# Attention heads of a two-block model: two waits of TensorE moved behind seven steps of projection, and the softmax division moved from VectorE to ScalarE

## The reference, cut to what matters

```
for layer in range(2):
    xn = rmsnorm(h, norm_mix[layer])
    if kind == 0:   # forget-gate attention, causal, with a bias c_q - c_k
        q, k, v, f_logit, qm = split(xn @ w_in_fox)
        p = softmax(q k^T * scale + c_q - c_k, masked)
    else:           # rotary positions, three dilated branches in one mask
        q, k, v, qm = split(xn @ w_in_dil)
        q, k = apply_rope(q), apply_rope(k)
        ...
    heads = concatenate([p @ v, memory_attention(qm, mem)])
    h = h + merge_heads(heads) @ w_out[layer]
    h = h + conv_ffn(rmsnorm(h, norm_ffn[layer]), ...)
```

## Time and profile before

| | |
|---|---|
| median of 3 timed runs | 2222.05 us (2220.85 to 2223.23) |
| the profiled execution's own time | 2216.38 us |
| its span | 2214.6 us |
| PE busy | 2099.2 us, 95% of the span |
| DVE busy | 1290.1 us, 58% |
| ACT busy | 466.4 us, 21% |
| POOL busy | 844.8 us, 38% |
| share of PE in the chain that ended last | 76%, of DVE 13%, of DMA 7% |

### The profile page before, as it was taken

How to read it: one execution, slowest core, us unless ns; L and a number is a source line. 1 busy time by engine, 2 the same in 40 slices (tenths; PEclk the granted TensorE clock), 3 DMA queues, 4 the chain that set the end, 5 groups by cost and what they waited for, 6 DMA issues and landing times.

```text
span 2214.6 us, 27273 instructions
## 1 busy us (share of the span) xinstructions
PE 2099.2 (95%) x10722; PEld 1669.6 (75%) x10722; DVE 1290.1 (58%) x1798; ACT 466.4 (21%) x852; POOL 844.8 (38%) x1008
## 2 busy tenths in 40 slices
PE   6999898998899999989999999999899999999996
PEld 4778786676788888867777888888676678888885
DVE  7686664448662342574565763727546757637274
ACT  3013301213210000123333210202233432102011
POOL 1333323233444444433222444444422324444442
PEclk7999999999999999999999999999999999999998
DMA  8978776589998988866665889898776648899885
GB/s 285 206 176 190 146 144 143 115 222 244 247 237 187 194 194 196 191 147 153 128 138 132 189 181 203 192 193 181 173 152 133 131 110 188 189 198 193 193 188 123
DMA packets 124615, 394.40 MB, mean 178 GB/s; under 512 B 26028, under 2 KB 28076, under 8 KB 124232
## 3 DMA queue, kind: packets, MB, share of 16 engines
q0 software_dynamic: 96480, 346.20, 72.5%
q1 hardware_dynamic: 28008, 46.45, 6.6%
HBM read 385.63 MB, written 3.94 MB: 176 GB/s over the span
## 4 chain that ended last, share of the span: by engine, by line
PE 76%; DVE 13%; DMA 7%; issue 1%; ACT 1%; SPq 1%; POOL 1%; DVEq 0%; ACTq 0%
PE ps L1674 65%; DMA w_lo<-in_w 4%; PE ps L1703 2%; PE ps L1870 2%; PE ps L1897 1%; PE ps L1883 1%; DMA arena<-in_ada 1%; DMA w_hi<-in_w 1%; DVE work L754 1%; PE ps L2062 1%; DVE small L927 1%; DVE arena L755 1%; DVE arena L637 1%; DVE arena L925 1%; POOL w_lo L497 1%
## 5 line engine op out<-in xcount | busy, mean ns | idle before, releaser
L1674 PE MATMUL ps<-h_hi,w_hi 128*128 128x512 f32 x1760 | 710.9, 404 | 36.6 <-DVE arena L862 14.4
L1674 PE MATMUL ps<-h_lo,w_hi 128*128 128x512 f32 x1760 | 690.7, 392 | 0.0
L1674 PE MATMUL ps<-h_hi,w_lo 128*128 128x512 f32 x1760 | 690.6, 392 | 0.0
L491 POOL DMA_DIRECT2D w_hi<-in_w x334 | 186.6, 559 | 1166.8 <-PE ps L1674 1032.3
L1674 PEld LDWEIGHTS ps<-h_hi,w_hi 128*128 128x128 f32 x1760 | 333.4, 189 | 129.3 <-issue 25.1
L1674 PEld LDWEIGHTS ps<-h_hi,w_lo 128*128 128x128 f32 x1760 | 333.1, 189 | 71.6
L497 POOL TENSOR_SCALAR w_lo<-w_hi 128x1024 fp32r<-128x1024 f32 (+1 forms) x334 | 360.0, 1078 | 69.5 <-DMA w_hi<-in_w 64.0
L1674 PEld LDWEIGHTS ps<-h_lo,w_hi 128*128 128x128 f32 x1760 | 333.8, 190 | 65.7 <-issue 1.9
L500 POOL DMA_DIRECT2D w_lo<-in_w x334 | 300.5, 900 | 105.8 <-POOL w_lo L497 105.8
L1674 PE MATMUL ps<-g_hi,w_hi 128*128 128x512 f32 (+1 forms) x728 | 286.1, 393 | 8.4 <-DMA w_lo<-in_w 6.1
L1674 PE MATMUL ps<-g_lo,w_hi 128*128 128x512 f32 (+1 forms) x728 | 281.5, 387 | 0.0
(11 more groups left out here) (376 smaller groups left out, 2134.4 us busy)
## 6 DMA issues: line engine op xcount, KB each, us to landing
w_hi<-in_w POOLq DMA_DIRECT2D x318, 512.0 KB, 3.9
w_lo<-in_w POOLq DMA_DIRECT2D x318, 512.0 KB, 5.6
arena<-in_ada SPq DMA_DIRECT2D x40, 512.0 KB, 8.2
w_hi<-in_w POOLq DMA_DIRECT2D x16, 384.0 KB, 3.3
w_lo<-in_w POOLq DMA_DIRECT2D x16, 384.0 KB, 5.0
x<-in_ada SPq DMA_DIRECT2D x8, 512.0 KB, 4.5
arena<-forget_sums SPq DMA_DIRECT2D x6, 512.0 KB
work<-arena SPq DMA_DIRECT2D x48, 64.0 KB, 3.3
```

Source lines behind the costliest of these rows:

```text
L491: pool.dma_start(w_hi[:, q % SLOTS, 0:n], A["w"][q][:, 0:n]).then_inc(S(f"high_in{q % SLOTS}"), 16)
L1674: mm = pe.matmul(bank, w[:, slot, cols], a(k), start=(k == 0 and i == 0), stop=(k == blocks - 1 and i == 2))
```

## The change: what it does

1. PE runs 7 steps (42 matmuls: all of q0, three quarters of k0) before it waits for banks 2 and 3, and `FIRST_STEPS` is (7, 4) in place of (2, 4). Five units lose their third step for it: 13, 17, 21, 25 and 29. The sum of the steps is 86 as before.
2. With that count q0 and k0 are both done "before unit 0". Their eviction has a new place, `evicted(-1)`, behind `top_of(0)` on DVE and behind `exponents(0)` on ACT; in the loop the evictions keep their place.
3. The wait for the mask is joined to the wait for the rotary table on DVE: both transfers now count on one semaphore, and the waits of DVE and PE on `mask_in` are gone.
4. The two multiplications of `divided` go from DVE (L935) to ACT, as Copy with a scale read per partition. DVE keeps the reciprocal and signals it. On ACT the division of unit u+1 stands behind `kept(u)`.

```diff
-FIRST_STEPS = (2, 4)
+FIRST_STEPS = (7, 4)
-    return 3 if u < 11 or u % 4 == 1 else 2
+    return 3 if u < 11 else 2
...
-            sp.dma_start(masks, A["mask_dil"]).then_inc(S("mask_in"), 16)
+            sp.dma_start(masks, A["mask_dil"]).then_inc(S("rope_in"), 16)
...
                 def divided(u):
-                    pair, qb, width, at = UNITS[u]
-                    pr, row = probs[u % P_SETS], small[:, 33 + u % P_SETS, :]
+                    row = small[:, 33 + u % P_SETS, :]
                     need("exped")
-                    do(dve.reciprocal(row[:, 2:4], row[:, 4:6]))
-                    for g in range(2):
-                        do(dve.tensor_scalar(pr[:, g, 0:width], pr[:, g, 0:width], row[:, 2 + g:3 + g], None, ALU.mult), "probs")
+                    do(dve.reciprocal(row[:, 2:4], row[:, 4:6]), "sums_turned")
...
                 top_of(0)
+                evicted(-1)
                 divided(0)
...
+                def divided(u):          # ScalarE
+                    width, row = UNITS[u][2], small[:, 33 + u % P_SETS, :]
+                    need("sums_turned")
+                    for g in range(2):
+                        pr = probs[u % P_SETS][:, g, 0:width]
+                        do(act.activation(pr, pr, ACT.Copy, scale=row[:, 2 + g:3 + g]), "probs")
...
                 exponents(0)
+                evicted(-1)
+                divided(0)
                 for u in range(len(UNITS) + 2):
...
+                    if u:
+                        evicted(u - 1)
                     if u < len(UNITS):
                         kept(u)
+                    if u + 1 < len(UNITS):
+                        divided(u + 1)
...
-                for at in (2, 3):
-                    pe.wait_ge(S(freed[at][0]), freed[at][1])
-                if layer:
-                    pe.wait_ge(S("mask_in"), 16)
                 steps = beside()
                 for _ in range(FIRST_STEPS[0]):
                     next(steps)
+                for at in (2, 3):
+                    pe.wait_ge(S(freed[at][0]), freed[at][1])
                 scores(0)
```

More of the change, by code:

```diff
@@ L852, in vector_layer @@
                 else:
-                    dve.wait_ge(S("rope_in"), 16)
+                    dve.wait_ge(S("rope_in"), 32)
                     for i in (2, 3):
@@ L867, in rotated @@
                     t, u = turn_room(1, i), work[:, 4, :]
-                    dve.wait_ge(S("rope_in"), 16 + 64 * (ROPED.index(name) + 1))
+                    dve.wait_ge(S("rope_in"), 32 + 64 * (ROPED.index(name) + 1))
                     do(dve.tensor_tensor(u, u, work[:, 3, :], ALU.mult))
@@ L904, in vector_layer @@
                 before = len(UNITS) * layer
-                if layer:
-                    dve.wait_ge(S("mask_in"), 16)
                 def pair_low(pair):
@@ L946, in beside, with evicted @@
                                 rotated(name)
+                    if u:
+                        evicted(u - 1)
+                def evicted(done):
                     for name, at in zip(BESIDE_PIECES, DONE_AT):
-                        if u == at + 1:
+                        if at == done:
                             if name[0] == "v":
@@ L1610, in kept, with evicted @@
                     do(act.activation(at_m["pt"][:, u % 2, :, 0:width], banks8[:, 4:6, 0:width], ACT.Copy), "probs_kept")
+                def evicted(done):
+                    for name, at in zip(BESIDE_PIECES, DONE_AT):
+                        if at == done:
+                            if name[0] == "v" or layer == 0:
+                                skip(1)
+                            else:
+                                rope_copy(name)
+                def divided(u):
[4 more added lines that the diff above has]
+                        do(act.activation(pr, pr, ACT.Copy, scale=row[:, 2 + g:3 + g]), "probs")
                 exponents(0)
+                evicted(-1)
+                divided(0)
                 for u in range(len(UNITS) + 2):
```

## The result

The changed kernel takes 2230.56 us (median of 5, 2226.07 to 2236.06) against 2223.23 for the kernel before beside it: 1.0039 times the time before, 95% interval 1.0024 to 1.0054. That is slower, where a gain of 8.3 us was forecast. The profiled execution is the shortest of the five, 2226.07 us; its span is 9.4 us longer than before.

What follows compares the result with a forecast made beforehand. PE's own work plus holes was taken as the bound. Layer 0 -9.3 us and layer 1 +1.0 sum to -8.3: 2208.1 for the profiled execution, 2213.7 us as timed median; own range 2210 to 2218, with rivals' bounds 2207 to 2221.

Steps and rivals of the forecast that it cites:

- (e): Layer 1 middle: idle from q and k swap waits and 512-wide units, 3.4 us again, so a change of 0.
- (d): Layer 1 middle: PE's clock falls once to its 1.2 GHz level behind a stall, +1.7 us (bounds 0 and 3).
- (b): Layer 1 middle: v0's first step waits for bank 0, freed by ACT's copy of q0 behind exponents(0), +2.5 us.
- (c): Layer 1 middle: q0 and k0 swapped back to back in loop 2, delaying unit 3's transposes, +4.4 us (bounds 3 and 6).
- (a): Layer 1 middle: three projection steps fewer, -4.2 us; the same -4.2 was booked in layer 0's middle.
- Layer 0's head: From PE's first possible projection step to scores(0): 42 matmuls fill the hole, scores(0) at 993.4 instead of 997.38, -4.0 us.
- the rule weighed in the prediction: DVE's divisions: two-port VectorE tensor_scalar and GpSimd lock each other out; moving them to ACT takes such blocks away.
- Layer 0's tail: From scores(25) to the last head block: two steps ahead -2.8, kept and slower division +1.0, together -1.8 us.
- The two steps ahead: Layer 0's tail: PE arrives with 70 steps done in place of 68, -2.8 us.
- ACT's price of the division: Division on ACT: 0.722 us for a 512-wide pass and 0.509 for 256, taken from Exp rows; DVE needs 0.491.
- ACT becomes the bound: Rival, chance 0.08: PE-ACT loop over 48 mixing units; 0.26 us more each is over 0.2% slower, 0.4 us ends at 2233.
- the gain is given back: Rival, chance 0.20: swap meets POOL, clock falls after both stalls; layer 1 costs 5, layer 0 gives 7: 2220 us.

Runs made afterwards that it cites:

- the second profile of the change: The unaltered change measured once more beside the kernel before, on the chip of that call: 2229.71 us, 1.0038 of the kernel before.
- the swaps' edit: The full change with a second buffer for the swapped halves, used in turn: 2217.34 us, 0.9983 of the kernel before.

## Why the prediction was wrong

**The step that failed** is (e) of layer 1's middle: "q1, k1, q2, k2 meet theirs in three-step loops with room", put down at 0. Each of these loops was costed by one question, whether the transposes of the probabilities would be late. But the count sets the evictions too. Before, v1 and v2 were evicted in loops 6 and 10, k1 and k2 rotated in loops 7 and 11. Now k1 is rotated and v1 evicted in loop 5, k2 and v2 in loop 9. The eviction is written behind the rotation, and PE's next projection but one waits for its bank. Before, v1's eviction stood behind a rotation too, that of q1 in loop 6, but q1's swap had landed and DVE didn't wait for it; the wait came a loop later, for k1, behind the eviction. DVE before:

```profile
1655.97 0.69 DVE L871 TENSOR_TENSOR arena<-arena,work 128x512 f32<-128x512 f32 x1
1656.69 0.69 DVE L877 TENSOR_TENSOR arena<-ps,work 128x512 f32<-128x512 f32 x1
...
1661.83 1.46 DVE L869 TENSOR_TENSOR work<-work 128x512 f32<-128x512 f32 x1 [2.55 <-DMA work<-arena]
```

Two such waits in PE were 3.35 and 4.34 us, and the clock behind them 5.1: 12.8 us where 0 stood. The two runs with one edit each show both halves of it: with the evictions first the wait goes to 0.2 us while DVE still waits for swaps, with a second buffer the middle returns to 148.85. The prediction asked what is queued behind DVE's waiting pass, and listed a take, a reciprocal, a division and the transposes for unit 3; it did not ask the same in loops 5 and 9. (k3, k4 and k5 share loops 13, 19 and 25 with v3, v4 and v5; there steps are two to a loop, and no wait for L877 is above 0.5 us.)

**(d) The clock** was counted once, 1.7 us. It fell behind three holes, for 2.6, 2.7 and 2.4 us: both the number of falls and the size of each were too small. In the second profile of the change it fell behind four.

**(b) and (c) were right**: 2.53 us for bank 0 against 2.5; 3.63 before the transposes of unit 3 against 4.0, for the reason given, as the swaps' edit shows, which takes it away.

**(a) Three steps fewer** in each middle were -4.2. With DVE's division layer 0's middle fell by 2.8 only. The rest went into three short waits for banks, for L862 at 997.3 us and for L877 at 1011.3 and 1061.3. Their idle time is 0.6 us (PE is busy 143.21 of 143.80), but the matmuls behind them start 0.48, 0.55 and 0.75 us after the ones before and the next ones 0.30, where the pace is 0.23: 1.3 us. The prediction had 0.1 for them. Layer 1's sum: 11.5 us more idle (15.0 against 3.4), 7.7 of clock, less 4.1 for the steps, are 15.1, against 15.9 measured; that a wait costs more than its idle time can be the rest.

**Layer 0's head**: -3.0 in place of -4.0. (That "the first ten or so matmuls" behind the old hole were 0.43 us apart was read too high: before, it is the first seven.) PE had done its seven steps and still waited 1.13 us for L862. In the chain of the norm one pass had become longer. The timeline of DVE and POOL after, where DVE's row took 0.47 us before:

```profile
987.76 1.78 DVE L888 TENSOR_SCALAR work<-work,vec 12x512 f32<-12x512 f32 x1
988.20 1.07 POOL L497 TENSOR_SCALAR w_lo<-w_hi 128x1024 fp32r<-128x1024 f32 x1
```

The pass takes 1.77 to 1.81 us in all ten profiles with the new head in layer 0 and 0.47 in the two without it, where no pass of POOL lies beside it. With 0.47 PE would hardly have waited. With PE at work, the weight stream goes on, and POOL's passes fall into what had been a quiet stretch. This is the behaviour of the rule weighed in the prediction, from its other side: the Trainium skill, "SBUF — State Buffer", section "Who interferes with whom". The trace agrees in that DVE's pass is the one that grows; which of POOL's instructions holds it (a DMA issue stands just before the L497 above) it doesn't show. The argument of the prediction, which used it only for the divisions, should have applied it to the head.

**Layer 0's tail**: +2.3 in place of -1.8. The term of kept and the slower division was +1.0 (bounds 0 and 4.4). Measured, the tail with DVE's division is 38.91 to 41.32, with ACT's behind the kept copy 42.07 to 42.56 at the same count of steps. Of the 2.75 us between the change and the run with DVE's division (39.75), 0.5 are idle time (3.7 against 3.2 before the transposes) and 1.6 clock. 0.6 are a wait inside the transposes: those of the second head stand until ACT has divided it, so that eight take 1.41 us at full clock in place of 1.06. The stalls of the tail with their transposes, first after, then before:

```profile
1153.67 1.41 PE L1899 MATMUL ps<-con,arena 128*128 128x128 f32 x8 [1.30 <-ACT arena L1626]
...
1172.20 1.83 PE L1899 MATMUL ps<-con,arena 128*128 128x128 f32 x8 [2.38 <-ACT arena L1626]
```

```profile
1179.21 1.06 PE L1883 MATMUL ps<-con,arena 128*128 128x128 f32 x8 [1.73 <-ACT arena L1610]
```

From the last of these rows to the end of the stage it is 6.92 us after and 4.99 before. The two steps ahead, put at -2.8, brought 0.5 with DVE's division (39.75, clock up): PE is busy 2.6 us less and idle 2.1 more, in stalls before the transposes of unit 27 and before the outputs. That a tail without cover turns work done early into waiting was said for the chain of the units, but the steps were still booked at full price. Layer 1's tail gave 0.5 and 1.6 in the two profiles of the change, for 3.1. Over all runs with the new count it took 39.99 to 43.52 us with DVE's division and 40.50 to 42.77 with ACT's, so there no price of the division shows.

**ACT's price of the division** was right, the Exp rows to 1%. In layer 0:

```profile
L1626 ACT ACTIVATE arena<-arena,small 128x512 f32<-128x512 f32 x12 | 8.7, 725 | 0.4
```

So was its cost in layer 0's middle: +0.6 predicted, +0.5 measured. The other page weighed, the Trainium skill's "ScalarE: Activation LUTs", section "Rules for kernel authors", would keep the multiplication on VectorE; with the head as before the move does cost (1.0026), mostly as a late link of the chain in layer 0's tail and not as work on ACT; with the holes gone layer 1 is shorter with it. The rival "ACT becomes the bound" (0.08) had the right sign and the wrong cause: it fails in the run of the head alone, which is slower without any work added to ACT. The nearest of the rivals was "the gain is given back", through holes with the clock behind them; it stopped at 5 us in layer 1 because it, too, looked only at the transposes.

**The size of the whole**: by stages the change is -3.0 + 14.9 = +11.9 us. The stretches that it doesn't touch came out 2.1 us shorter up to layer 0's stage in this execution, and the span rose by 9.4; the medians rose by 7.3, the ratio says 8.7 (5.3 to 12). The head alone is +7.3 us by its ratio and the division alone +5.8, more than the 8.7 of both; by stages it is 7.0 and 4.2 against 11.9. With intervals some 3 us wide to each side that is no proof that the two parts work on each other.

**Open**: whether the division costs anything on ACT once the holes are gone (by stages 3.9 us in layer 0 against 3.6 gained in layer 1, part of both through the clock; by time nothing that can be told), and why the change with the division ahead of the copy is 13 to 20 us slower in six of its seven executions than in the one profiled.

## What to carry to other kernels

When a schedule counts steps to place its work, a shift of the count re-pairs everything that hangs on it: list for each loop which in-order queue now holds a wait on a transfer and which bank's release stands behind it. Put what frees TensorE's banks ahead of what waits for a transfer. Price a hole in TensorE with the clock that may fall behind it (in the change 1.4 to 2.7 us each time), and book work moved ahead of an uncovered tail at what the tail's chain lets through, not at its own time.

## What was not expected of the hardware

Whether the clock falls behind a hole doesn't follow from the hole's length alone. In layer 1 after, PE was granted 1.2 GHz behind holes of 3.35 to 4.34 us, not behind one of 2.53 at the stage's head. The same hole of 2.53 us stands in seven profiles, and the clock fell behind it in two, the second profile of the change and the one with evictions first. In the run with two swap buffers it fell behind 2.41 (0.84 from 1679 to 1690). In layer 0's tail it fell behind, or during, the stall of 2.38 to 2.40 us in all six runs with ACT's division behind the kept copy, and in none behind the 1.30 to 1.32 us before it. With DVE's division the same stall of 1.72 or 1.73 us was followed by transposes of 1.06 us in four runs and 1.57 in one, and a stall of 1.45 to 1.48 by 1.06 in two and 1.94 in one: the tails with the new head are 38.9 and 39.8 us where it stayed up, 41.3 where it fell.
